# Neighbourhood attention: the negated maximum from one fused instruction, own PSUM banks for the second head's transposes, and four groups of factor transposes at other steps

## The reference

```python
def neighborhood_attention(q, k, v, rpb, scale):
    ...
    def one(r):
        r0 = jnp.clip(r - kr // 2, 0, rows - kr)
        ...
        bias = rpb[:, dr[:, None, None], dc[None, :, :]]
        s = jnp.einsum('bchd,brcjhd->bhcrj', q_r, k_r, preferred_element_type=jnp.float32) * scale
        s = s + bias.transpose(0, 2, 1, 3)[None].astype(jnp.float32)
        p = jax.nn.softmax(s.reshape(B, H, GRID_W, kr * kc), axis=-1).reshape(B, H, GRID_W, kr, kc)
        return jnp.einsum('bhcrj,brcjhd->bchd', p.astype(v.dtype), v_r)
```

## Time and profile before

| What | Value |
|---|---|
| median of 3 runs | 3879.32 us (3878.24 to 3884.2) |
| profiled execution, span from first to last instruction | 3882.8 us |
| PE busy over the span | 3787.5 us, 98% |
| DVE, ACT, POOL busy | 2660.0, 1931.0, 660.4 us |
| mean granted TensorE clock | 0.994 |

### The profile page before, as it was taken

The page is one execution under the profiler, slowest core; times in us unless marked ns, Lnnn a source line. Parts: engine busy times, 40 slices in busy tenths (PEclk is TensorE's granted clock), DMA queues, the critical chain, the costliest instruction groups (busy, mean ns, idle before and its releaser), DMA issues.

```text
span 3882.8 us, 53821 instructions
## 1 busy us (share of the span) xinstructions
PE 3787.5 (98%) x21662; PEld 2942.4 (76%) x21662; DVE 2660.0 (69%) x3327; ACT 1931.0 (50%) x2848; POOL 660.4 (17%) x747
## 2 busy tenths in 40 slices
PE   8999999999999999999999999999999999999999
PEld 5876667887876667887843668888888888888887
DVE  4346967675436967534345664989889859898898
ACT  5336866324336866324356443544445655444454
POOL 1120121011120121011058831000001430000010
PEclk9999999999999999999999999999999999999999
DMA  5332000453332000232100001121111111111111
GB/s 209 93 95 53 1 1 12 174 213 102 95 92 53 1 1 35 97 122 76 44 12 1 26 33 65 55 76 44 55 64 57 44 44 60 61 44 55 65 55 65
DMA packets 67735, 247.55 MB, mean 64 GB/s; under 512 B 15648, under 2 KB 16288, under 8 KB 55456
## 3 DMA queue, kind: packets, MB, share of 16 engines
q1 hardware_dynamic: 53648, 193.51, 14.8%
q10 hardware_dynamic: 13840, 50.60, 3.5%
HBM read 206.34 MB, written 29.36 MB: 61 GB/s over the span
## 4 chain that ended last, share of the span: by engine, by line
PE 82%; DVE 8%; ACT 4%; issue 3%; POOL 2%; DMA 1%; DVEq 0%; ACTq 0%; POOLq 0%
PE ps L1786 31%; PE ps L1042 13%; PE ps L1294 3%; PE ps L1296 3%; PE ps L1295 3%; PE ps L1474 2%; PE ps L1157 2%; PE ps L1190 2%; PE ps L1532 2%; PE ps L1521 2%; PE ps L1426 1%; PE ps L1442 1%; PE ps L1412 1%; PE ps L1175 1%; PE ps L1576 1%
## 5 line engine op out<-in xcount | busy, mean ns | idle before, releaser
L1786 PE MATMUL ps<-x_piece1hi,w_piece1hi 128*128 128x512 f32 x672 | 262.4, 390 | 0.2 <-DVE x_piece1lo L3523 0.2
L1786 PE MATMUL ps<-x_piece0hi,w_piece0hi 128*128 128x512 f32 x672 | 262.3, 390 | 0.0
L1786 PE MATMUL ps<-x_piece0hi,w_piece0lo 128*128 128x512 f32 x672 | 261.5, 389 | 0.0
L1786 PE MATMUL ps<-x_piece1hi,w_piece1lo 128*128 128x512 f32 x672 | 261.5, 389 | 0.0
L1786 PE MATMUL ps<-x_piece0lo,w_piece0hi 128*128 128x512 f32 x672 | 261.4, 389 | 0.0
L1786 PE MATMUL ps<-x_piece2hi,w_piece2lo 128*128 128x512 f32 x672 | 261.4, 389 | 0.0
L1786 PE MATMUL ps<-x_piece1lo,w_piece1hi 128*128 128x512 f32 x672 | 261.4, 389 | 0.0
L1786 PE MATMUL ps<-x_piece2hi,w_piece2hi 128*128 128x512 f32 x672 | 261.4, 389 | 0.0
L1786 PE MATMUL ps<-x_piece2lo,w_piece2hi 128*128 128x512 f32 x672 | 261.4, 389 | 0.0
L1042 PE MATMUL ps<-n_hi_m,w_lo 128*128 128x512 f32 x576 | 225.5, 392 | 0.0
L4045 POOL TENSOR_TENSOR rope_cos<-rope_cos,arena 128x512 f32<-128x512 f32 x42 | 65.4, 1556 | 734.1 <-ACT arena L2497 731.2
(11 more groups left out here) (514 smaller groups left out, 10727.8 us busy)
## 6 DMA issues: line engine op xcount, KB each, us to landing
w<-in_wstream SPq DMA_DIRECT2D x87, 1024.0 KB, 5.1
arena<-in_wstream SPq DMA_DIRECT2D x40, 1024.0 KB, 5.0
arena<-in_wstream ACTq DMA_DIRECT2D x16, 1024.0 KB, 5.2
n_saved<-n_hi_m SPq DMA_DIRECT2D x16, 512.0 KB, 7.3
n_saved<-n_lo SPq DMA_DIRECT2D x16, 512.0 KB, 8.3
n_hi_h<-n_saved SPq DMA_DIRECT2D x16, 512.0 KB, 8.0
n_lo<-n_saved SPq DMA_DIRECT2D x16, 512.0 KB, 9.1
out<-h ACTq DMA_DIRECT2D x32, 256.0 KB, 2.2
```

What stands on the lines that cost most here:

```text
L1786: last = mm(dst[:, e, :], a_part[:, pair, k, f], b_part[:, k, :], start=(n in FRESH and half == 0 and k == 0 and t == 0), stop=(half == 1 ...
```

## The change

Three things are changed in the NA stage.

1. `top` works on the negated sum with a minimum in place of a maximum, so the fused instruction leaves the negated maximum itself. The second, small instruction and the wait before it are gone. ACT undoes the sign with a scale of -1.
2. The second head's transposes go to bank 7, and their fifth tile to columns 128 to 255 of bank 6. A unit's transposes then wait for the evacuation of the unit two before (`pt_act` to u - 1), no longer for that of the one before, and no longer for `pt_dve`. Those of the second head of an inner step wait on `o_free` instead.
3. The factor transposes use bank 5 and stand at steps 14, 15 (pair 0) and 22, 23 (pair 1).

```diff
+NA_FACTORS_AT = {NT * (hp + 1) + NT - 2 + hf: (hp, hf) for hp in range(NA_H // 2 - 1) for hf in range(2)}
+
+
+def _na_turned(u, b):
+    return ((7, 0) if b < NA_W // P else (6, P)) if u % 2 else (4 + b // 4, 0)
...
                     def probs_t(u):
                         pe.wait_ge(sems["exp_done"], T.since("exp_done", u + 1))
-                        if u:
-                            pe.wait_ge(sems["pt_act"], T.since("pt_act", u))
-                        if u and u % 2 == 0:
-                            pe.wait_ge(sems["pt_dve"], T.since("pt_dve", NA_INNER_AT[u // 2]))
-                        for b, size in key_tiles(NA_PAIRS[u // 2][3]):
-                            last = nc.tensor.transpose(ps[0:size, 4 + b // 4, (b % 4) * P:(b % 4) * P + P],
-                                                       na_p_of(u)[:, b * P:b * P + size], ident)
+                        inner = NA_PAIRS[u // 2][3]
+                        if u >= 2:
+                            pe.wait_ge(sems["pt_act"], T.since("pt_act", u - 1))
+                        if inner and u % 2:
+                            pe.wait_ge(sems["o_free"], T.since("o_free", u // 2))
+                        for b, size in key_tiles(inner):
+                            bank, at = _na_turned(u, b)
+                            at += b % 4 * P
+                            last = nc.tensor.transpose(ps[0:size, bank, at:at + P], na_p_of(u)[:, b * P:b * P + size], ident)
...
-                        factor_turns(hp, hf, 7)
+                        factor_turns(hp, hf, 5)
...
-                        if s > NT and s % NT in (3, 4):
-                            factors(s // NT - 1, s % NT - 3)
+                        if s in NA_FACTORS_AT:
+                            factors(*NA_FACTORS_AT[s])
...
-                        nc.scalar.activation(x, x, ACT.Exp, bias=negm[:, u:u + 1], accum_out=sums[:, u:u + 1])\
+                        nc.scalar.activation(x, x, ACT.Exp, scale=-1.0, bias=negm[:, u:u + 1], accum_out=sums[:, u:u + 1])\
...
-                            na_inner[hp][:, j, :] if inner else na_bias[hp % 2][:, j, e * GW:e * GW + NA_W], 1.0, 4 * MASKED, ALU.add, ALU.max, mx[:, u:u + 1])\
-                            .then_inc(sems["v_link"], 1)
-                        dve.wait_ge(sems["v_link"], T.next("v_link"))
-                        V.tensor_scalar(negm[:, u:u + 1], mx[:, u:u + 1], -1.0, None, ALU.mult)\
+                            na_inner[hp][:, j, :] if inner else na_bias[hp % 2][:, j, e * GW:e * GW + NA_W], -1.0, -4 * MASKED, ALU.add, ALU.min, negm[:, u:u + 1])\
                             .then_inc(sems["m_ready"], 1)
...
-                        V.tensor_copy(na_pt_of(u)[0:GW, NA_W:NA_K], ps[0:GW, 5, 0:NA_K - NA_W]).then_inc(sems["pt_dve"], 1)
+                        V.tensor_copy(na_pt_of(u)[0:GW, NA_W:NA_K], ps[0:GW, 6, P:2 * P]).then_inc(sems["pt_dve"], 1)
...
-                        if s > NT and s % NT in (3, 4):
-                            normed_out(s // NT - 1, s % NT - 3)
+                        if s in NA_FACTORS_AT:
+                            normed_out(*NA_FACTORS_AT[s])
```

More of the change, by code:

```diff
@@ L2256, in evacuate @@
                         width = NA_K if u % 2 == 0 and NA_PAIRS[u // 2][3] else NA_W
-                        nc.scalar.activation(na_pt_of(u)[:, 0:width], psf[:, 4 * HALF:4 * HALF + width], ACT.Copy)\
+                        at = _na_turned(u, 0)[0] * HALF
+                        nc.scalar.activation(na_pt_of(u)[:, 0:width], psf[:, at:at + width], ACT.Copy)\
                             .then_inc(sems["pt_act"], 1)
@@ L3182, in normed_out @@
                         dve.wait_ge(sems["o_free"], T.since("o_free", NT * (hp + 1)))
-                        out_times(hp, hf, 7)
+                        out_times(hp, hf, 5)
                     def out_times(hp, hf, bank):
```

## The result

| | before | after |
|---|---|---|
| median | 3880.07 us of 4 runs (3878.24 to 3884.2) | 3910.98 us of 4 runs (3907.39 to 3914.21) |
| profiled execution | span 3882.8 us | 3910.09 us, span 3907.9 us |

The ratio is 1.008, 95% interval 1.0067 to 1.0092: the change costs 30.9 us (26 to 36 by the interval). The page shows where it isn't: PE is as busy as before and DVE has 96 instructions and 16 us less.

What follows compares the result with a forecast made beforehand. The prediction took PE to bound the NA stage. Added waits 12.7, pauses 18.0 and lower clock 8.0, less gains of 2 x (0.3 + 0.3 + 0.4), make 36.7 us: 3879.3 + 36.7 = 3916, range 3901 to 3926.

Steps and rivals of the forecast that it cites:

- What bounds the stage: NA stage: PE alone is the bound, busy 84.7 of 85 us, its matmuls waiting 0.2 us in all.
- The rival of a loop bound by `top`: Inner steps: scores, tops and scores are the true bound, so fusion saves some 18 us, giving 3861; chance 0.03.
- Part 2, 24 x 0.53 = 12.7 us: Inner steps: second head's transposes wait for `out`'s copy of the values, 0.53 us for each of 24 waits.
- Part 3, the pause of 9.0 us twice: Hand-over to pair 2: its bias load waits for pair 0's later factors, so PE stands still 9.0 us a layer.
- The clock, 8.0 us: Behind the pause: the granted clock falls to 0.50 and work runs at half speed, 4 us a layer.
- The rival that the clock holds: At the pause: the clock holds or recovers before work resumes, sum without 8.0, giving 3908; chance 0.20.
- The gains, 2.0 us: Each layer: 0.3 us at the stage's start, 0.3 for step 12 and its like, 0.4 from pair 1's factors.
- the wait at step 12: Transposes at step 12 wait 0.18 us for DVE's fifth-tile copy; dropping this and its like gains 0.3 us a layer.
- the 0.73 us at the end: Stage's end: PE waits 0.73 us for unit 45's banks; one group of pair 1's factors is hidden there.

Runs made afterwards that it cites:

- Experiment 1: The kernel before with the fused negation alone, banks and factors as before: 3880.25 us, ratio 0.9996.
- experiment 4: The changed kernel with pair 0's reciprocals spread into free weight tiles, so pair 2's bias load no longer waits for the factors: 3890.72 us, ratio 1.0026.
- experiment 5: The changed kernel with the second head's fifth tile in bank 3 and the bias load freed from pair 0's factors: 3878.24 us, ratio 0.9997.
- Experiment 3: The changed kernel with the second head's fifth tile in columns 128 to 255 of bank 3 instead of bank 6: 3897.97 us, ratio 1.0045.
- Experiment 2: The kernel before with the factor transposes moved to steps 14, 15, 22 and 23 alone, still in bank 7: 3905.24 us, ratio 1.0064.
- experiment 6: The changed kernel with PE's pause filled by 44 warm-up products that nobody reads: 3908.55 us, ratio 1.0075.

## Why the prediction was right

The forecast was 3916 with 3901 to 3926, the result 3910.98. The mechanism held in both places, one term was mis-sized, and the small gains came from other places than forecast.

- **What bounds the stage.** Right: PE alone. Experiment 1 takes the 96 small instructions out and the stage stays at 88.69 us. The rival of a loop bound by `top` falls.
- **Part 2, 24 x 0.53 = 12.7 us.** Right in kind and size. In the row of the step above the copy ends at 283.98 and the transposes start 0.14 later, and the transposes start 0.75 us after the last value product where the prediction said 0.7. Comparing experiments 4 and 5, which differ in the bank alone and have no pause, gives 94.15 - 87.89 = 6.26 us a layer, 12.5 in all, or 0.52 for each wait. By the rule that the prediction cited, the Trainium skill (PSUM — Partial Sum Buffer, "PSUM bank collisions raise a hardware error"), these 12.5 us are the price of a guarded bank. Experiment 3 keeps that guard and still pays nothing, since it writes to a bank whose reader is done in any case. Whether the wait could simply be dropped in bank 6, as the addresses alone allow, was not tried.
- **Part 3, the pause of 9.0 us twice.** Right step by step: factors 0.66, SP's issue 0.69 behind their start (331.59 to 332.28), the bias in use at 8.3 (339.86, predicted 8.5), the scores at 9.64 (341.23, predicted 10.2, the two tops and PE's release taking 1.37 in place of 1.69); only `top` stood idle a little longer than the 7 to 9 us forecast, 9.99. PE's gap is 8.82 us in the first layer and 9.16 in the second where transposes and scores stand 0.20 apart elsewhere: 8.6 and 9.0, together 17.6 against 18.0. Experiment 2 shows that the moved factors alone make it; experiment 4, which leaves them at the new steps and takes away SP's wait for them, has no pause.
- **The clock, 8.0 us: the mis-sized term.** "If the clock falls 2 to 5 us into it and stays down as long, 6.7 to 9.7 us of work run at half speed": it did fall in the pause, some 2.7 us into it, inside the 2 to 5 that the prediction assumed without a row for it. What failed is "stays down as long": it was down for 10.2 us (6.0 + 4.2), not for the 13.7 of the earlier gap, and most of that lay in the pause itself. So only 4.2 us of work in the first layer ran at half clock (3.6 in the second). From `scores(17)` to the next scores it takes 5.20 and 4.96 us where experiment 6 has 3.26: 1.95 and 1.70 more, so 3.65 us in place of 8.0. The rival that the clock holds falls too; by its time, 3908, it was nearer than the forecast (3.0 us off against 5.0), and only the windows tell the two apart.
- **The gains, 2.0 us.** Right in size: 0.3 us a layer at the start (experiment 1), 0.8 in the stage for step 12 and the end (experiment 5) against 0.7. The split of the 0.7 was wrong, so it is partly luck that the sum came out right. Experiment 2 has the factors alone: the wait at step 12, which the prediction gave to the banks, is gone there, and the 0.73 us at the end, which was to hide a group of factors, is still waited for. Less its pause (9.1 and 9.2 us) and its slow clock (1.8 and 2.5), its stage is some 88.4 us, 0.2 under before, where the prediction had 0.4. The other 0.6 of the 0.8 came with the banks, at the end of the stage, where the prediction put nothing for them: PE's wait there is 0.25 in place of 0.73.

With measured terms the sum is 12.5 + 17.6 + 3.65 - 2.2 = 31.6 us; the medians differ by 30.9. Nothing of size is left over.

## What to carry to other kernels

When code is moved, look at what waits for its semaphore on the queues that aren't in the diff: four transposes, which lengthen a step by 0.44 us wherever they stand (4.45 against 4.01 at step 11 before, 4.06 against 3.62 at step 14 after), cost 20 us here because a load of another table waits for them; with another place for what they read, so that the load need not wait, the pause was gone. A buffer that is split off to loosen one wait must not land beside one that another engine reads at that moment: ask for each bank who reads it last, and put the tile where that reader is done anyway. Where PE is the bound, instructions that are saved on another engine are worth what they take off PE's own waits, here 0.6 of 14 us.

## What the runs showed of the hardware

Two pauses of the same kind did not cost the same clock. In the changed kernel's first layer it was down by the window that starts at 335.20, some 2.7 us after the last transposes, and 4.2 us of work fell into the slow stretch; in experiment 3, with a pause about as long (PE's gap is 8.65 us, against 8.82), it was still 1.00 in the window that ends 4 us into it, and 5.9 us of work fell into it. The loss was 1.95 and 2.75 us. The other four pauses of that kind agree: gaps of 9.16 (changed kernel, second layer), 9.05 (experiment 3), 9.29 and 9.38 us (experiment 2) lost 1.70, 2.33, 1.83 and 2.46, each counted from `scores(17)` to the next scores, less 3.26. What a pause costs in clock is thus not fixed by its length, and a difference of 0.8 us between two kernels can come from that alone. Filling the pause with products that nobody reads kept the clock whole, for 1.8 and 2.0 us a layer; this agrees with the rule that the prediction cited, the Trainium skill (TensorE: Matmul & The Clock Gate, "The HAM clock gate"), that activity is what releases the throttle.
